# Another order of the block products, and the last units of the MLP's second token half behind the last group

## What is computed

```
hm = rms_norm(x, g_pre_mlp[i])
f = jnp.square(jax.nn.relu(hm @ w_mlp_up[i])) @ w_mlp_down[i]      # 1024 -> 4096 -> 1024
x = x + rms_norm(f, g_post_mlp[i])
gate = jax.nn.sigmoid(rms_norm(x, g_pre_ple[i]) @ w_ple_gate[i])
x = x + rms_norm(gate * (p[i] @ w_ple_proj[i]), g_post_ple[i])
```

## Time and profile before

| | |
|---|---|
| Median of 3 runs | 2764.78 us (2764.25 to 2767.42) |
| The profiled execution | 2765.39 us, span 2763.6 us |
| TensorE busy | 2697.1 us (98%), 12816 matmuls |
| VectorE busy | 2041.0 us (74%) |
| ScalarE busy | 1395.6 us (50%) |
| GpSimd busy | 291.1 us (11%) |
| Chain that ended last | PE 90%, DVE 6%, ACT 1%, DMA 1% |

### The profile page before, as it was taken

The page is one execution under the profiler, slowest core; times in us unless marked ns, Lnnn a source line. Parts: engine busy times, 40 slices in busy tenths (PEclk is TensorE's granted clock), DMA queues, the critical chain, the costliest instruction groups (busy, mean ns, idle before and its releaser), DMA issues.

```text
span 2763.6 us, 34607 instructions
## 1 busy us (share of the span) xinstructions
PE 2697.1 (98%) x12816; PEld 2242.8 (81%) x12816; DVE 2041.0 (74%) x2767; ACT 1395.6 (50%) x2399; POOL 291.1 (11%) x329
## 2 busy tenths in 40 slices
PE   8999999999999999989999999999999999999897
PEld 7878888888888888867888788888888888888685
DVE  5468888385777777788866688883767777777886
ACT  5337888464333333346644478884633333333473
POOL 0320000001111111100013200000010111111000
PEclk9999999999999999999999999999999999999998
DMA  4211112431111111132332111143311111112332
GB/s 163 78 57 48 33 34 95 157 111 65 62 54 54 54 39 57 58 136 85 106 113 76 51 40 34 29 146 120 137 39 48 60 62 51 51 38 67 123 106 76
DMA packets 86519, 208.28 MB, mean 75 GB/s; under 512 B 9040, under 2 KB 37840, under 8 KB 85328
## 3 DMA queue, kind: packets, MB, share of 16 engines
q1 hardware_dynamic: 86352, 206.07, 22.1%
HBM read 174.52 MB, written 31.52 MB: 75 GB/s over the span
## 4 chain that ended last, share of the span: by engine, by line
PE 90%; DVE 6%; ACT 1%; issue 1%; DMA 1%; POOL 0%; SPq 0%; DVEq 0%; ACTq 0%
PE ps L1093 27%; PE ps L1095 27%; PE ps L1094 27%; PE ps L1299 4%; PE ps L1324 2%; PE ps L1323 2%; DVE wl L2067 1%; DVE xf L2489 1%; DVE nm L2303 1%; DMA raw<-w_units 1%; DVE xf L2121 1%; PE ps L1132 0%; PE ps L1133 0%; DVE ptl L2310 0%; DVE xf L2124 0%
## 5 line engine op out<-in xcount | busy, mean ns | idle before, releaser
L1093 PE MATMUL ps<-hh,wh 128*128 128x512 f32 x2160 | 850.5, 394 | 15.6 <-DVE hl L2103 8.2
L1094 PE MATMUL ps<-hl,wh 128*128 128x512 f32 x2160 | 843.2, 390 | 0.0
L1095 PE MATMUL ps<-hh,wl 128*128 128x512 f32 x2160 | 843.0, 390 | 0.0
L1588 ACT ACTIVATE wh<-raw 128x256 fp32r<-128x256 f32 (+1 forms) x522 | 324.4, 639 | 429.9 <-PE ps L1095 273.3
L2067 DVE TENSOR_TENSOR wl<-raw,wh 128x256 fp32r<-128x256 f32 (+1 forms) x522 | 400.6, 787 | 142.3 <-ACT wh L1588 141.6
L1093 PEld LDWEIGHTS ps<-hh,wh 128*128 128x128 f32 x2160 | 407.4, 189 | 103.6 <-issue 11.6
L1094 PEld LDWEIGHTS ps<-hl,wh 128*128 128x128 f32 x2160 | 407.3, 189 | 87.1 <-issue 3.4
L1095 PEld LDWEIGHTS ps<-hh,wl 128*128 128x128 f32 x2160 | 407.1, 188 | 85.1
L2489 DVE TENSOR_TENSOR xf<-xf,ps 128x1024 f32<-128x1024 f32 x280 | 338.5, 1214 | 62.0 <-PE ps L1095 61.6
L1093 PE MATMUL ps<-hx,wh 128*128 128x512 f32 x448 | 174.3, 389 | 0.0
L1094 PE MATMUL ps<-hx,wh 128*128 128x512 f32 x448 | 174.3, 389 | 0.0
(11 more groups left out here) (233 smaller groups left out, 4252.0 us busy)
## 6 DMA issues: line engine op xcount, KB each, us to landing
raw<-w_units SPq DMA_DIRECT2D x182, 512.0 KB, 3.4
raw<-w_units SPq DMA_DIRECT2D x112, 256.0 KB, 2.9
x_mid<-xf SPq DMA_DIRECT2D x4, 2048.0 KB, 8.0
xf<-x_mid SPq DMA_DIRECT2D x4, 2048.0 KB, 8.3
hh<-mix_hi SPq DMA_DIRECT2D x14, 512.0 KB, 6.2
hl<-mix_lo SPq DMA_DIRECT2D x14, 512.0 KB, 7.2
stage<-w_head SPq DMA_DIRECT2D x16, 320.0 KB, 3.3
mix_hi<-cyh SPq DMA_DIRECT2D x8, 512.0 KB, 2.6
```

What stands on the lines that cost most here:

```text
L1093: nc.tensor.matmul(dst, ah, bh, start=start, stop=False)
L1094: nc.tensor.matmul(dst, ah, bl, start=False, stop=False)
L1095: return nc.tensor.matmul(dst, al, bh, start=False, stop=stop)
L1588: return nc.scalar.activation(dst, src, ACT.Copy, **more)
```

## The change

`TURNS` takes the products in the order 1, 7, 5, 6, 2, 3, 4 instead of 1, 2, 3, 5, 6, 7, 4, in all seven big groups. `SUM_ORDER` of GpSimd, the banks and the steps follow. A product of the first pair waits only for the hidden parts of its own k, no longer for all fourteen. In the last big group the products follow directly on the fourth unit; all four last units of token half 1 stand behind the 28 products, their weights are loaded behind the four quarters, and `post_stats` of half 0 moves one unit earlier. ScalarE and VectorE get the first three joins and squares of half 0 inside the product phase (`LAST_ACT`, `LAST_DVE`), and the steps behind are rearranged. The saved `x` of half 0 is fetched two loads earlier.

```diff
-QUARTER_LOADS = [[M_BIG + 8 * G + (5 if G + 1 < BIG else 6) + i for i in range(QUARTERS)] for G in range(BIG)]
-U_LAST = (M_BIG + 8 * BIG - 4, M_BIG + 8 * BIG + 2)
+QUARTER_LOADS = [[M_BIG + 8 * G + (5 if G + 1 < BIG else 4) + i for i in range(QUARTERS)] for G in range(BIG)]
+U_LAST = (M_BIG + 8 * BIG, M_BIG + 8 * BIG + 2)
...
-TURNS = [(pair, k) for pair in (0, 2) for k in (1, 2, 3, 5, 6, 7, 4)]
+TURNS = [(pair, k) for pair in (0, 2) for k in (1, 7, 5, 6, 2, 3, 4)]
...
-SUM_ORDER = [(0, 5), (0, 7), (0, 6), (1, 5), (1, 7), (1, 6), (0, 4), (1, 4),
+SUM_ORDER = [(0, 5), (1, 5), (0, 7), (1, 7), (0, 6), (1, 6), (0, 4), (1, 4),
...
-HOME_BEFORE = [D_LAST[1], PLE_AT + 1]
+HOME_BEFORE = [D_LAST[0], PLE_AT + 1]
...
-    return (4, 6, 2, 0)[turn % 4] if G + 1 < BIG else (4, 6, 2)[turn % 3]
+    return (4, 6, 2, 0)[turn % 4]
...
+use.0 part.7 use.1 part.8 use.2 part.9 use.3 part.10 use.4 part.11 use.5 part.12 use.6 part.13 part.14 use.7 part.15
...
+LAST_ACT = [(("part", 22), ("square_down", 0, 0)), (("part", 23), ("square_down", 0, 1)),
+            (("part", 24), ("square_down", 0, 4)), (("part", 25), ("square_down", 0, 5))]
+LAST_DVE = [(("use", 9), ("whole", 0)), (("part", 25), ("sum_down", 0, 1)), (("part", 26), ("sum_down", 0, 4)),
+            (("part", 27), ("sum_down", 0, 5)), (("use", 18), ("whole", 1))]
...
-    at = kept.index(("hidden", 1, 6)) + 1
-    kept.insert(at, early[0])
-    kept.insert(at + 2, ("unit", 6))
-    at = kept.index(("hidden", 1, 3)) + 1
-    return kept[:at] + early[1:] + kept[at:]
+    at = kept.index(("hidden", 1, 7)) + 1
+    kept[at:at] = early
+    kept.remove(("unit", 4))
+    kept.insert(kept.index(("part", 27)) + 1, ("unit", 4))
+    for before, step in LAST_ACT if order is BIG_ACT else LAST_DVE:
+        kept.insert(kept.index(before) + 1, step)
+    return kept
...
-    ("up", 31, 1): [("post", 1, 0)],
+    ("up", 30, 0): [("post", 1, 0)],
...
-                    if n == 0:
-                        pe.wait_ge(big_lo, hidden_at(L, G, *HIDDEN_ORDER[-1]))
+                    if i == 0:
+                        pe.wait_ge(big_lo, max(hidden_at(L, G, c, o) for c in range(2) for o in (k, TURNS[0][1])))
...
-                        if g:
-                            pe.wait_ge(down_add, used_at(L, BIG - 1, len(TURNS) - 1))
+                        if i == 0:
+                            pe.wait_ge(down_add, used_at(L, BIG - 1, max(o for o in range(len(TURNS)) if banks_of(BIG - 1, o) == 2 * g)))
...
-                    else:
-                        last_units(0)
                     for n in range(MADE):
                         product(G, n)
+                last_units(0)
                 last_units(1)
```

More of the change, by code:

```diff
@@ L270 @@
 sum.1.6 hidden.1.5 hidden.1.6 part.1 part.2 part.3 part.4 part.5 part.6 value.3.0 hidden.1.2 sum.1.3 hidden.1.3
-value.4.1 value.4.0 use.0 part.7 use.1 part.8 use.2 part.9 part.10 use.3 part.11 part.12 use.4 part.13 use.5
-part.14 use.6 part.15 part.16 use.7 part.17 use.8 part.18 use.9 part.19 part.20 use.10 part.21 use.11 part.22
-use.12 part.23 part.24 use.13 part.25 part.26 use.14 part.27 use.15 use.16 unit.5 use.17 use.18 use.19
+value.4.1 value.4.0
+use.0 part.7 use.1 part.8 use.2 part.9 use.3 part.10 use.4 part.11 use.5 part.12 use.6 part.13 part.14 use.7 part.15
+part.16 use.8 part.17 part.18 use.9 part.19 part.20 use.10 part.21 use.11 part.22 use.12 part.23 use.13 part.24 use.14
+part.25 use.15 part.26 use.16 part.27 use.17 unit.5 use.18 use.19
 """)
 MLP_ACT = steps("""
-hidden.30.0 square_down.0.0 square_down.0.1 hidden.30.1 square_down.0.2 square_down.0.3 square_down.0.4 square_down.0.5
-square_down.0.6 square_down.0.7 high.100 hidden.31.0 high.101 post.1.0 high.102 hidden.31.1 chunk.1.0.0 high.103
-chunk.1.0.1 chunk.1.0.2 square_down.1.0 chunk.1.0.3
-square_down.1.1 chunk.1.0.4 high.104 chunk.1.0.5 chunk.1.0.6 high.105 chunk.1.0.7 high.106 square_down.1.2
+square_down.0.2 square_down.0.3 square_down.0.6 square_down.0.7 high.98 hidden.30.0 post.1.0 hidden.30.1 high.99
+chunk.1.0.0 high.100 chunk.1.0.1 hidden.31.0 high.101 chunk.1.0.2 hidden.31.1 high.102 chunk.1.0.3 chunk.1.0.4 high.103
+chunk.1.0.5 square_down.1.0 chunk.1.0.6 square_down.1.1 chunk.1.0.7 high.104 high.105 high.106 square_down.1.2
 embed.0 square_down.1.3 embed.1 high.107 embed.2 pre.1.0 embed.3 high.108 embed.4 square_down.1.4 embed.5
@@ L293 @@
 MLP_DVE = steps("""
[L294 to L299 removed]
+sum_down.0.2 sum_down.0.3 sum_down.0.6 sum_down.0.7 whole.2 value.30.0 low.98 rest.30.0 whole.3 add_x.1.0.0 value.30.1
+add_x.1.0.1 rest.30.1 low.99 add_x.1.0.2 low.100 value.31.0 sum_chunk.1.0.1 add_x.1.0.3 rest.31.0 add_x.1.0.4
+sum_chunk.1.0.2 low.101 value.31.1 sum_chunk.1.0.3 add_x.1.0.5 rest.31.1 low.102 sum_chunk.1.0.4 add.31.0 add_x.1.0.6
+add.31.1 low.103 add.31.2 sum_chunk.1.0.5 add_x.1.0.7 chunk.1.0.0 chunk.1.0.1 sum_chunk.1.0.6 chunk.1.0.2 add.31.3
+sum_down.1.1 chunk.1.0.3 add.31.4 sum_chunk.1.0.7 chunk.1.0.4 add.31.5 low.104 chunk.1.0.5 low.105 chunk.1.0.6 low.106
+add.31.6 sum_down.1.2 chunk.1.0.7 add.31.7 sum_down.1.3
 low.107 low.108 sum_down.1.4 sum_down.1.5 sum_down.1.6 low.109 sum_down.1.7 low.110 z.0 add_x.1.1.0 low.111
@@ L425 @@
         SQUARES += squares_of_in(layer, out)
-    for order in (MIX_ACT, mlp_order(layer, MLP_ACT)):
+    for order in (MIX_ACT, [step for _, step in LAST_ACT], mlp_order(layer, MLP_ACT)):
         SQUARES += squares_of(layer, order)
@@ L2052, in big_steps @@
                             big_unit(G, *n)
+                        elif kind == "square_down":
+                            down_square(*n)
                 big_square(0, 0, 1)
@@ L2516, in big_steps @@
                             big_unit(G, *n)
+                        elif kind == "whole":
+                            whole(*n)
+                        elif kind == "sum_down":
+                            add_square((L, "post", 1) + tuple(n))
                 def gate_value(n):
```

24 lines of the change are left out of this document (9 added, 15 removed).

## The result

| | before | after |
|---|---|---|
| Median, side by side | 2765.66 us (2764.25 to 2769.16) | 2777.7 us (2777.08 to 2779.33) |
| Ratio, 95% interval | | 1.0043 (1.0028 to 1.0058) |
| Span of the profiled execution | 2763.6 us | 2777.5 us |

The changed kernel is slower by 12 us. The forecast was no change, 2763.6 us in a range of 2751 to 2773. TensorE's waits in the whole span, in the columns of the earlier trace rows. The lines are 7 to 9 higher: the low parts of weights (before L2067) are L2076, the uses (L2489) L2498, and the additions of `two_groups` (L2441) L2450.

What follows compares the result with a forecast made beforehand. TensorE, busy throughout the first six big groups, bounds the kernel, so gains lie only behind the last group. Sum: -2 x 1.6 (tail) + 2 (twelve groups) = -1.2 us, giving 2763.6 us, no change; range 2751 to 2773.

Steps and rivals of the forecast that it cites:

- the six groups: First six big groups of each layer: no gain, a small loss, 2 us in twelve groups over both layers.
- the fourth quarter comes at 16.9: Six first big groups: the fourth quarter's weight load is there 16.9 us behind the group's first product.
- the slack: Ends of the six groups: next unit's low part ready at 37.95, wanted at 38.08; slack shrinks from 3 us to 0.1.
- 0 to 11 us for the twelve groups: Bounds on the twelve groups' loss; 11 if each comes 0.9 late like the landing of 1187.34; 2 taken.
- the six groups lose their slack: Slower rival: load behind part 26 makes each of twelve groups 0.7 us later, 9.6 us in all, 2771.2 us; chance 0.23.
- the tail's 3.2 us: Behind the last big group: the embedding starts 1.6 us earlier in each of two layers.
- The last group: From P (end of its fourth unit): VectorE late, 5 us newly lost, products end at 43.1 instead of 38.1.
- the lock: Slower rival, last group: four GpSimd sums fully block VectorE, 2 us later per layer, 2767.6 us; chance 0.05 within no change.
- Behind it: Tail behind the last group's products: TensorE waits 3.7 us for a use and 5.9 for unit 102; statistics don't wait.
- The clock: Behind the 3.7 us wait ahead of the last units: TensorE's matmuls run at half clock, costing 2.5 us.
- VectorE keeps up: Faster rival, last group and tail: VectorE in time; one gain gives 2756.6 us, both 2749.5; chance 0.27.

Runs made afterwards that it cites:

- e4_part12_earlier: Changed kernel with only part 12 one use earlier in VectorE's order in every big group, part 13 left in place; 2767.09 us, ratio 1.0004 to the kernel before.
- e2_tail_only: Changed kernel with the old order of products, sums and VectorE's steps back in the first six big groups; 2765.67 us, ratio 0.9995 to the kernel before.
- e9: Changed kernel with part 13 straight behind part 12 in VectorE's order, no use between them; 2770.27 us, ratio 1.0012 to the kernel before.
- e3: Changed kernel with parts 12 and 13 each one use earlier in VectorE's order in every big group; 2764.03 us, ratio 0.9995 to the kernel before.
- e5: e3 with chunk 3's sum and a residual step behind unit 102's low part on VectorE; 2756.32 us, ratio 0.9967 to the kernel before.
- e6: e3 with five of the last group's seven first parts moved from ahead of `value.3.1` into VectorE's waiting gaps; 2758.15 us, ratio 0.9973 to the kernel before.
- e8: Edits of e3, e5 and e6 together, half 0's statistics one output later, VectorE's and ScalarE's steps to suit; 2751.46 us, ratio 0.9949 to the kernel before.
- e10: e8 with three more places moved in the tail's lists, such as `use.17` ahead of `unit.4`; 2748.19 us, ratio 0.9932 to the kernel before.

## Why the prediction was wrong

**The step that failed** is one term of the six groups: "the fourth quarter comes at 16.9". It was a load of 3.6 us behind part 13, as in the kernel before, where the two loads are issued 2.4 us apart. The new order issues them 1.5 us apart, and then the second takes 4.5: it comes at 17.8. The walk around it was right to 0.1 us (part 12 at 11.8, third quarter at 15.3), and so was the slack: 0.1 us. A microsecond into a slack of 0.1, twelve times, is the result. e4_part12_earlier, in which the fourth quarter does come at 16.9, loses the 2.0 us that I had summed.

**I took the wrong end of my bounds, and the far one was too near.** I gave 0 to 11 us for the twelve groups and chose 2, "since most landings lie near the short end"; it was 12.4, for the microsecond came twelve times and each restart cost some tenths more. They do where nothing is close ahead of them. The row of 1187.34, 4.5 us, didn't show this effect: it was the third quarter of the last group, and in the kernel before SyncE issues nothing else from 1170 up to it. That its 4.5 us are the time which the fourth quarter's load takes in the new order is luck. What lies beside it is a transfer of the queue that brings instructions, 0.4 us behind its issue (SyncE's row, then that queue's from 1183 to 1184):

```profile
1182.84 3.26 SPq L925 DMA_DIRECT2D raw<-w_units  x4
```

```profile
q8 instruction: 1, 0.02, 8.5%
```

What the loss cost was forecast as a rival, "the six groups lose their slack", with the right place (the load behind part 26) and the right point from which it decides (38.08), at 2771.2. It was 0.8 us for each group in that sum and is 1.0, and the tail's 3.2 us, which I took off, did not come. A range to 2773 left out its own bound: 2764.8 - 3.2 + 11 is 2772.6 only with the tail's gain in it, and 2776 without.

**The last group.** `value.3.1` at P - 1.3 (P - 1.3), `use.0` at P + 8.6 (8.6), part 12 at 17.4 (17.5), TensorE's wait ahead of product 14 1.34 (1.7), the end of the products at 43.5 (43.1), the first of the last units at 46.9 (46.8): measured in layer 0, and forecast in brackets. So the lock didn't decide either: with four whole GpSimd sums `value.3.1` would have been 2 us later than it was.

**Behind it** the two long waits came as forecast, 3.3 (3.7) released by a use and 5.9 (5.9) released by unit 102. Two things did not, in layer 0. The clock: I charged 2.5 us behind the first wait. In the changed kernel the granted clock stayed at 1.00 there (the stretch 1214 to 1220), so the unit was done at P + 52.5 instead of 54.8, and the statistics, which I had waiting for nothing, waited 2.1 us for sums that end at 54.7 (54.0). Behind *that* wait the clock fell to 0.53, the 1.2 GHz level. So the time saved behind the first wait was spent on a second one and on the clock behind it, and `value.31.1` was at 75.9 instead of 74.1. In layer 1 the first wait was 3.8, the matmuls behind it took 1.7 us more, and the statistics waited 0.4; `value.31.1` was at 75.3. In the two kernels with just this last group and tail (after and e2_tail_only, two layers each) P to the embedding is 102.6 to 104.4, on average 103.2; I had 101.8, and before it is 103.2 too. (Where parts 12 and 13 were moved it is 102.0 to 103.0 in e4 and e9, and 100.6 and 101.6 in e3.) The tail's gain was not 1.6 us a layer but nothing that can be told from noise, and so nothing was left to set against the groups.

**The rival "VectorE keeps up"** fell: VectorE's share of idle time in the tail was real, but not where its queue needs it. It took changes of the queue's order to use it (e5, e6, e8, e10).

## What to carry to other kernels

Where an engine has no idle time, the slack of each deadline is the number to work out, and a slack of 0.1 us times twelve groups is a loss in waiting: price it with the slow end of each transfer on its way. When a change moves the issue of two transfers closer together, the second (and at 0.9 us the first too) can take longer, as here; take its duration from a row with the same distance to the one ahead, not from the median. And an instruction that waits for another engine should stand behind everything in its queue that is ready and that the bounding engine needs: moving one sum and one step behind unit 102 gave 7.7 us, more than the whole change had in view.
